# GLA + HGRN2 decoder step: the order of the prologue around the first projection unit

## The reference

```python
def rms_norm(x, w):
    xf = x.astype(jnp.float32)
    y = xf * lax.rsqrt(jnp.mean(xf * xf, axis=-1, keepdims=True) + EPS)
    return (y * w.astype(jnp.float32)).astype(x.dtype)
...
m, s_gla_new, s_hg_new = token_mix(rms_norm(x, norm_mix_pre[l]), w_in[l], ...)
    proj = h @ w_in_l                       # 1024 x 9232, split into 11 parts, one the rank-16 gate
    ... two gated linear recurrences (GLA, 4 heads; HGRN2, 8 heads), gates, merged @ w_out_l
h = x + rms_norm(m, norm_mix_post[l])
f = swiglu(rms_norm(h, norm_ffn_pre[l]), w_ffn_in[l], w_ffn_out[l])
return h + rms_norm(f, norm_ffn_post[l]), s_gla_new, s_hg_new
```

## Time and profile before

| | us |
|---|---|
| Median of 3 runs | 1066.75 (1066.43 to 1067.47) |
| The profiled execution | 1066.12 |
| Its span, first to last instruction | 1064.3 |
| TensorE busy | 1043.1 |
| VectorE busy | 676.6 |
| ScalarE busy | 467.8 |
| POOL busy | 72.4 |

### The profile page before, as it was taken

How to read it: one execution, slowest core, us unless ns; L and a number is a source line. 1 busy time by engine, 2 the same in 40 slices (tenths; PEclk the granted TensorE clock), 3 DMA queues, 4 the chain that set the end, 5 groups by cost and what they waited for, 6 DMA issues and landing times.

```text
span 1064.3 us, 24323 instructions
## 1 busy us (share of the span) xinstructions
PE 1043.1 (98%) x10640; PEld 962.5 (90%) x10640; DVE 676.6 (64%) x982; ACT 467.8 (44%) x720; POOL 72.4 (7%) x89
## 2 busy tenths in 40 slices
PE   7999999999999999999999999799999999999997
PEld 5988999989999899999899878799999999888886
DVE  6266635675526765356664589998888888744544
ACT  6433344622536233445325447544444444533532
POOL 5200003000003000030000020000000000000000
PEclk9999999999999999999999999999999999999999
DMA  6522213622227322245222372123324232422212
GB/s 193 168 72 81 76 55 109 190 62 81 70 62 213 86 62 81 71 124 163 73 61 91 97 250 60 41 80 110 89 83 117 79 106 74 139 80 79 79 60 89
DMA packets 130777, 105.25 MB, mean 99 GB/s; under 512 B 4272, under 2 KB 115888, under 8 KB 130672
## 3 DMA queue, kind: packets, MB, share of 16 engines
q1 hardware_dynamic: 125808, 85.88, 27.4%
q0 software_dynamic: 4864, 17.83, 5.5%
HBM read 91.89 MB, written 11.80 MB: 97 GB/s over the span
## 4 chain that ended last, share of the span: by engine, by line
PE 89%; DVE 5%; ACT 2%; DVEq 1%; issue 1%; ACTq 1%; DMA 0%; POOL 0%; SPq 0%; POOLq 0%
PE ps L282 34%; PE ps L1880 21%; PE ps L1904 13%; PE ps L1171 10%; PE ps L1073 2%; PE ps L1104 1%; PE ps L1094 1%; PE ps L1106 1%; PE ps L1111 1%; PE ps L1087 1%; PE ps L1143 1%; DVE h_t L931 1%; PE ps L1069 1%; PE ps L1131 0%; PE ps L1057 0%
## 5 line engine op out<-in xcount | busy, mean ns | idle before, releaser
L268 ACT ACTIVATE w_hi_t<-w_raw_t 128x1024 fp32r<-128x1024 f32 x73 | 77.2, 1058 | 302.9 <-PE ps L282 218.1
L272 DVE TENSOR_TENSOR w_lo_t<-w_raw_t,w_hi_t 128x1024 fp32r<-128x1024 f32 x73 | 89.7, 1229 | 168.0 <-ACT w_hi_t L268 167.6
L282 PE MATMUL ps<-x_hi,w_lo_t 128*128 128x288 f32 x896 | 195.8, 300 | 0.0
L282 PE MATMUL ps<-x_hi,w_hi_t 128*128 128x288 f32 x896 | 191.5, 295 | 0.0
L282 PE MATMUL ps<-x_lo,w_hi_t 128*128 128x288 f32 x896 | 191.1, 295 | 0.0
L282 PEld LDWEIGHTS ps<-x_hi,w_lo_t 128*128 128x128 f32 x896 | 143.0, 188 | 4.4 <-issue 2.5
L282 PEld LDWEIGHTS ps<-x_lo,w_hi_t 128*128 128x128 f32 x896 | 143.9, 188 | 0.0
L282 PEld LDWEIGHTS ps<-x_hi,w_hi_t 128*128 128x128 f32 x896 | 143.9, 188 | 0.0
L1880 PE MATMUL ps<-x_hi,w_lo_t 128*128 128x288 f32 x264 | 78.1, 296 | 3.5 <-DVE work L1696 2.4
L1880 PE MATMUL ps<-x_lo,w_hi_t 128*128 128x288 f32 x264 | 77.8, 295 | 0.0
L1880 PE MATMUL ps<-x_hi,w_hi_t 128*128 128x288 f32 x264 | 77.8, 295 | 0.0
(11 more groups left out here) (313 smaller groups left out, 2262.7 us busy)
## 6 DMA issues: line engine op xcount, KB each, us to landing
w_raw_t<-in_w_in_dram SPq DMA_DIRECT2D x57, 512.0 KB, 3.7
merged<-in_w_ffn_in_dram SPq DMA_DIRECT2D x22, 512.0 KB, 5.1
w_raw_t<-in_w_ffn_in_dram SPq DMA_DIRECT2D x22, 512.0 KB, 4.5
w_raw_t<-in_w_ffn_out_dram SPq DMA_DIRECT2D x22, 512.0 KB, 3.7
w_raw_t<-in_w_in_dram SPq DMA_DIRECT2D x32, 256.0 KB, 3.8
h_t<-in_x_prompt_dram SPq DMA_DIRECT2D x8, 512.0 KB, 5.3
h_t<-in_state_gla_dram POOLq DMA_DIRECT2D x4, 1024.0 KB, 6.2
h_t<-in_state_hgrn_dram POOLq DMA_DIRECT2D x8, 512.0 KB, 8.0
```

The source lines that it names most:

```text
L268: nc.scalar.activation(w_hi_t[:, u % NSPL, 0:nk, :], w_raw_t[:, u % NRAW, 0:nk, :], ACT.Copy).then_inc(w_hi, 1)
L272: nc.vector.tensor_tensor(w_lo_t[:, u % NSPL, 0:nk, :], w_raw_t[:, u % NRAW, 0:nk, :], w_hi_t[:, u % NSPL, 0:nk, :].bitcast(F32), ALU.subt ...
L282: m = nc.tensor.matmul(out[:, q, :], w[:, u % NSPL, k, :], x(k, q), start=first and i == 0, stop=last and i == len(todo) - 1)
```

## The change

- The norm row is made by eight transposes on TensorE of the gain column, spread to 128 columns, straight into `gain_rows`. VectorE's product and the matmuls with ones go.
- Tile 1 is squared and summed on VectorE (`square_1`, into the same `stat` column), the others still on ScalarE. Tiles 1 and 2 share one Ln and one Exp over two columns.
- Tile 2's rounded copy and remainder are cut in two parts: the first 32 tokens (they complete the first half of 288), and the other 96. There are now six parts (`X_PARTS`), and the banks of the transposed tiles change (`X_BANK`).
- TensorE runs the first half of the low-rank unit after the transposes of tiles 0 to 2, then transposes tiles 3 and 4, then runs the first half of unit 1, the second half of low rank, and the second half of unit 1. Unit 1 leaves the units' loop. One group of four small matmuls stays, ahead of low rank.
- ScalarE and VectorE are written out to match.
- SP issues the two weight loads ahead of tiles 3 and 4.

```diff
+X_BANK = (0, 4, 2, 0, 6)
+X_PARTS = ((0, 0, P), (1, 0, P), (2, 0, HT - 2 * P), (2, HT - 2 * P, P), (3, 0, P), (4, 0, TS))
+NX = len(X_PARTS)
+FIRST_X = 3
...
         for c in range(NT):
+            if c == 3:
+                load_unit(sp, 0, win_v[:, :, GLR:GLR + P])
+                load_unit(sp, 1, win_v[:, :, UNITS[0][0]:UNITS[0][0] + P])
             sp.dma_start(xt[c][0:tok(c), :], xp_v[c] if c < NC else xs_v).then_inc(x_in[c], 16)
-        load_unit(sp, 0, win_v[:, :, GLR:GLR + P])
-        load_unit(sp, 1, win_v[:, :, UNITS[0][0]:UNITS[0][0] + P])
...
+        def main_part(i):
+            act.wait_ge(turned, X_PARTS[i][0] + 1)
+            act.activation(x_hi[:, :, x_cols(i)], x_turned(i), ACT.Copy).then_inc(x_hi_s, 1)
+
+        square_sum(0)
+        inverse_root(0, 1)
+        square_sum(2)
+        act.wait_ge(sum_1, 1)
+        inverse_root(1, 3)
+        main_part(0)
+        square_sum(3)
+        inverse_root(3, 4)
+        main_part(1)
+        main_part(2)
+        square_sum(NC)
+        inverse_root(NC, NT)
+        act.wait_ge(x_lo_s, FIRST_X)
+        main_part(3)
+        main_part(4)
+        main_part(5)
...
-        dve.tensor_tensor(gains, ident[:, :].rearrange("p (o n) -> p o n", o=1).broadcast_to([P, KT, P]),
-                          gain[:, 0, :].rearrange("p (k o) -> p k o", o=1).broadcast_to([P, KT, P]), ALU.mult).then_inc(gain_diag, 1)
+        dve.wait_ge(x_in[1], 16)
+        dve.drain()
+        dve.scalar_tensor_tensor(square_1, xt[1], 1.0, xt[1], ALU.mult, ALU.mult, accum_out=stat[:, 0, 1:2]).then_inc(sum_1, 1)
         dve.wait_ge(gain_row, 1)
...
+        scale_x(0)
+        scale_x(1)
+        scale_x(2)
+        rest_part(0)
+        rest_part(1)
+        rest_part(2)
+        scale_x(3)
+        scale_x(NC)
+        rest_part(3)
+        rest_part(4)
+        rest_part(5)
...
-        for k in range(2):
-            m = nc.tensor.matmul(gain_rows[:, k * HALF:(k + 1) * HALF], ones[:, :], gains[:, 4 * k:4 * k + 4, :], start=True, stop=True)
+        for k in range(KT):
+            m = nc.tensor.transpose(gain_rows[:, k * P:(k + 1) * P], gain[:, 0, k:k + 1].broadcast_to([P, P]), ident[:, :])
         m.then_inc(gain_row, 1)
...
+        def first_unit(q):
+            for k in range(KT):
+                for n, (w, x) in enumerate(((w_lo_t, xh), (w_hi_t, xl), (w_hi_t, xh))):
+                    m = nc.tensor.matmul(proj(1)[:, q, :], w[:, 1, k, :], x(k, q), start=k == 0 and n == 0, stop=k == KT - 1 and n == 2)
+            return m
+
+        turn_x(0)
+        turn_x(1)
+        turn_x(2)
+        pe.wait_ge(x_lo_s, 1)
+        for _ in range(4):
+            nc.tensor.matmul(ps[:, 0, 0:P], ones[:, :], ones[:, :], start=True, stop=True)
+        pe.wait_ge(w_lo, 2)
+        pe.wait_ge(x_lo_s, FIRST_X)
+        low_rank(0)
+        turn_x(3)
+        turn_x(NC)
+        pe.wait_ge(x_lo_s, FIRST_X + 1)
+        pe.wait_ge(w_lo, 3)
+        first_unit(0)
+        pe.wait_ge(x_lo_s, NX)
+        low_rank(1).then_inc(unit_done, 1)
+        first_unit(1).then_inc(unit_done, 1)
```

More of the change, by code:

```diff
@@ L339, in turned_x @@
     def turned_x(c):
-        return ps[:, 2 * (c % 3):2 * (c % 3) + 2, :].rearrange("p a b -> p (a b)").rearrange("p (k t) -> p k t", k=KT)[:, :, 0:tok(c)]
+        bank = X_BANK[c]
+        if c == NC:
+            return ps[:, bank, :].rearrange("p (k t) -> p k t", k=KT)
+        return ps[:, bank:bank + 2, :].rearrange("p a b -> p (a b)").rearrange("p (k t) -> p k t", k=KT)
     def tokens(c):
@@ L552, in _, with square_sum, inverse_root @@
         act.wait_ge(setup, SETUP)
[L553 to L565, removed]
+        def square_sum(c):
+            n = tok(c)
+            act.wait_ge(x_in[c], 16)
+            act.activation(square[0:n, :], xt[c][0:n, :], ACT.Square, accum_out=stat[0:n, 0, c:c + 1])
+        def inverse_root(c0, c1):
+            n = tok(c0)
+            act.drain()
+            act.activation(stat[0:n, 1, c0:c1], stat[0:n, 0, c0:c1], ACT.Ln, scale=1.0 / D, bias=eps_c[0:n, :])
+            act.drain()
+            act.activation(stat[0:n, 1, c0:c1], stat[0:n, 1, c0:c1], ACT.Exp, scale=-0.5).then_inc(squared, c1 - c0)
+        def main_part(i):
[17 more added lines that the diff above has]
+        main_part(5)
         act.wait_ge(small, 16 * 8)
@@ L767, in _, with scale_x, rest_part @@
         dve.drain().then_inc(merged_s, 1)
-        dve.wait_ge(consts, 5)
-        dve.wait_ge(gain_in, 16)
-        dve.tensor_tensor(gains, ident[:, :].rearrange("p (o n) -> p o n", o=1).broadcast_to([P, KT, P]),
-                          gain[:, 0, :].rearrange("p (k o) -> p k o", o=1).broadcast_to([P, KT, P]), ALU.mult).then_inc(gain_diag, 1)
-        dve.wait_ge(gain_row, 1)
[L773 to L782, removed]
+        def scale_x(c):
+            n = tok(c)
+            dve.wait_ge(squared, c + 1)
+            dve.scalar_tensor_tensor(xt[c][0:n, :], xt[c][0:n, :], stat[0:n, 1, c:c + 1], gain_rows[0:n, :],
+                                     ALU.mult, ALU.mult).then_inc(scaled, 1)
+        def rest_part(i):
+            dve.wait_ge(x_hi_s, i + 1)
+            dve.tensor_tensor(x_lo[:, :, x_cols(i)], x_turned(i), x_hi[:, :, x_cols(i)].bitcast(F32), ALU.subtract).then_inc(x_lo_s, 1)
+        dve.wait_ge(x_in[1], 16)
+        dve.drain()
+        dve.scalar_tensor_tensor(square_1, xt[1], 1.0, xt[1], ALU.mult, ALU.mult, accum_out=stat[:, 0, 1:2]).then_inc(sum_1, 1)
+        dve.wait_ge(gain_row, 1)
+        scale_x(0)
[9 more added lines that the diff above has]
+        rest_part(5)
         dve.wait_ge(small, 16 * 8)
@@ L1018, in _, with turn_x @@
     def _(pe):
-        pe.wait_ge(gain_diag, 1)
+        pe.wait_ge(gain_in, 16)
         pe.wait_ge(consts, 5)
-        for k in range(2):
-            m = nc.tensor.matmul(gain_rows[:, k * HALF:(k + 1) * HALF], ones[:, :], gains[:, 4 * k:4 * k + 4, :], start=True, stop=True)
+        for k in range(KT):
+            m = nc.tensor.transpose(gain_rows[:, k * P:(k + 1) * P], gain[:, 0, k:k + 1].broadcast_to([P, P]), ident[:, :])
         m.then_inc(gain_row, 1)
-        for c in range(NT):
+        def turn_x(c):
             n = tok(c)
-            if c >= 3:
-                pe.wait_ge(x_lo_s, c - 2)
-                for _ in range(4):
-                    nc.tensor.matmul(ps[:, 3 * (c - 3), 0:P], ones[:, :], ones[:, :], start=True, stop=True)
             pe.wait_ge(scaled, c + 1)
@@ L1033, in _, with low_rank @@
             m.then_inc(turned, 1)
-        pe.wait_ge(w_lo, 2)
-        for q in range(2):
-            pe.wait_ge(x_lo_s, 3 if q == 0 else NT)
+        def low_rank(q):
             for k in range(KT):
@@ L1040, in _ @@
                                          start=k == 0 and x is x_lo, stop=k == KT - 1 and x is x_hi)
-        m.then_inc(unit_done, 1)
+            return m
[3 more added lines that the diff above has]
+                    m = nc.tensor.matmul(proj(1)[:, q, :], w[:, 1, k, :], x(k, q), start=k == 0 and n == 0, stop=k == KT - 1 and n == 2)
+            return m
+        turn_x(0)
[15 more added lines that the diff above has]
+        first_unit(1).then_inc(unit_done, 1)
         def do_step(j, name):
@@ L1178, in _ @@
                 value_unit(j, n - V0)
-            elif j < G:
+            elif 0 < j < G or j == 0 and n > 0:
                 u = j * NU + n + 1
@@ L1183, in _ @@
                 unit_passes(u, proj(u), xh, xl).then_inc(unit_done, 1)
-            elif n < 3:
+            elif j == G and n < 3:
                 pe.wait_ge(unit_free, UB)
```

10 lines of the change are left out of this document (6 added, 4 removed).

## The result

Over 21 interleaved runs each, the changed kernel has a median of 1068.90 us (1067.51 to 1069.95), the kernel before 1066.86 (1066.18 to 1067.91). The medians lie 2.0 us apart; the ratio, 1.0017 (1.0011 to 1.0023), makes it 1.8 us: a small loss, clear of zero. The time forecast was 1067.4, in a range of 1065.3 to 1069.4.

A forecast was written before the change was run, and what follows sets the result against it. It took TensorE's matmul queue as the bound, so only the second unit's start counts: 29.2 - 28.54 = +0.7 us on the median of 1066.75 gave 1067.4 us, in a range of 1065.3 to 1069.4.

The forecast's parts named there:

- What bounds the kernel: TensorE's matmul queue: gain or loss is the shift of the second unit's start, 28.54 us in the profile before.
- Part 1: Norm row and tile 1's square on VectorE: first scaling at 7.55 instead of 7.66, 0.1 us, worth nothing unless ScalarE keeps up.
- Part 2: ScalarE's order: it idles to 7.5 for tile 2; the first rounded copy runs from 9.95 to 10.95.
- rival B: Clock at 1.2 GHz when low rank starts: its first half costs 2.16 us more, total +2.7, 1069.4; chance 0.22.
- Part 3: Transfers: behind both weight loads tile 3 lands at 12.8 (11.8 to 13.3), where ScalarE wants it at 10.9.
- Part 4: Chain from tile 3: low rank 17.2, unit 1's first half 20.8 (break-even 20.14), then 8.40 us to second unit at 29.2.
- rival C: TensorE: matmuls of unit 1's two halves run slower than whole units, at most 0.2 us; given little chance.
- The cover of the second half: Low rank's second half is wanted at 23.9, its last remainder done at 23.4: wait covered by only 0.5 us.
- low rank's first half, 2.16 us at the full clock: TensorE: low rank's first 16 matmuls, ahead of the transposes of tiles 3 and 4, take 2.16 us.
- the forecast case: Tile 3 landing at 11.8 to 13.3 with the full clock: 1066.4 to 1067.9 us; chance 0.55.
- Rival A: Tile 3 lands before ScalarE wants it at 10.9: second unit at 27.3, -1.2 us, 1065.5; chance 0.18.

The follow-up runs named there:

- e4: The kernel before with only the norm row changed to eight transposes: 1066.82 us, ratio 1.0001.
- e5: The changed kernel with ScalarE's copies of tile 1 and of tile 2's first 32 tokens ahead of tile 3's square: 1066.12 us, ratio 0.9997.
- e2: The changed kernel with SP's transfers in the old order, all token tiles before the two weight loads: 1066.29 us, ratio 0.9995.
- e3: The changed kernel with the old norm row (VectorE's product, two 512-column matmuls with ones): 1069.14 us, ratio 1.0022.
- e7: The changed kernel with the old order of transfers and nine matmuls with ones behind the norm row: 1065.75 us, ratio 0.9992.
- e6: The changed kernel with ten instead of four matmuls with ones ahead of low rank: 1068.20 us, ratio 1.0014.
- e1: The changed kernel with nine matmuls with ones behind the norm row and ten instead of four ahead of low rank: 1067.68 us, ratio 1.0009.
- e9: The same kernel as e7, timed once more on another chip: 1066.07 us, ratio 0.9993.
- e8: e7 with e5's order of copies on ScalarE: 1065.71 us, ratio 0.9992.
- e10: e5 with nine matmuls with ones behind the norm row, new order of transfers kept: 1065.92 us, ratio 0.9995.

## Why the prediction was right, and where its size was off

- **What bounds the kernel.** Right: the shift of the second unit's start, +2.90, is the span's +3.0. Nothing behind it moved between these two profiles (1035.8 and 1035.9 us to the end). Over all profiles here that stretch is 1035.7 to 1036.5 us, so from one execution to another a start tells the time only to within 0.8 us.
- **Part 1.** Right: the new row alone changes nothing (e4). VectorE squares tile 1 as forecast, and the first scaling starts at 7.69 where 7.55 was said.
- **Part 2.** The first copy was put at 9.95 and ran at 11.03. Here the clock was missed: "transposes of tile 0 end 1.1 after its scaling" is a full-clock figure from the earlier trace rows, and at the lower clock they take 1.97 (e5's profile has them apart). It was hidden under the wait for tile 3, as rival B said.
- **Part 3, the decision.** Right: tile 3 lands at 13.13 for 12.8, and ScalarE waits there. One reading was off: POOL first read the second weight load at 13.94, for its rounding, not at 15.06, and only from there does a limit of about 13.3 follow. e2 and e5 show that this wait, by transfer or by the place of the square, is the whole loss.
- **Part 4.** Low rank at 17.58 for 17.2. From there the sum had 2.16 for its first half, 3.65 came (+1.49); 1.4 for the transposes, 1.6 came (22.84 less 21.23); 8.40 to the second unit, 8.60 came, which is rival C below. With 0.38 for the late start these add up to 2.3; between 29.2 and 31.44 lie 2.24. The cover of the second half held: its matmuls follow at 26.11 without a hole.
- **The term that was mis-sized** is "low rank's first half, 2.16 us at the full clock", taken as the likely case at 0.55, with B at 0.22. Both cases are there, in the same kernel: ten runs of 21 lost 1.0 us (forecast 0.7), eleven lost 2.6 (rival B: 2.7). The median is the fastest run of the upper group, so one run the other way would have made it 1068.59. It lies outside the times of the forecast case (1066.4 to 1067.9); what kept it in the range is that the range reached up to B, and where between the two groups a median of such runs falls is luck. B's price was right in total and not in its parts: its 2.0 for the slow first half no run shows, the runs showed 1.49, and the late start, the transposes and unit 1 made up the rest. Its chance should have been about a half.
- **B's cause was wrong.** It was put on the missing long matmuls and a clock that has not risen by 17.2. The clock had risen by 14.23 and fell behind 17.40. e3 has the long matmuls and keeps both groups; e2, e5 and e7, without them, start low rank at full speed. The fall goes with the idle time ahead of low rank: with 2.29 and 2.90 us about half of the runs are slow, with 1.70 (e6) one at most of eleven, and with 1.1 or less there no profile shows it. That its length alone decides isn't shown: in e1 the clock fell earlier on, around holes of 1.21 and 0.87 us, and in e9, the same early work with holes of 2.06 and 0.78, it held. What the change costs besides is the transposes at the lower clock: e7, with the early matmuls, starts low rank 1.25 us sooner than e2. The long matmuls alone don't cure that (e3).
- **Rival A** (tile 3 not late) didn't happen, but e2 makes it happen: -1.2 was forecast, -0.6 measured, and -0.9 with the clock raised early (e7).
- **Rival C** happened, at the 0.2 us that it was given at most. The two halves of unit 1 take 3.27 and 3.20 us (22.84 to 26.11 and 28.24 to 31.44), not 3.12, and with low rank's 2.13 between them that is the 8.60. Whether the three weight tiles of one half are the reason isn't shown.

Open: the link of each group to the speed of low rank rests on one profile in each group, of two kernels (the changed one at 0.997, e3 at 0.999), and on the clock in the records of the other runs. Why the same idle time ends at either clock from run to run isn't shown. Also open is why e5, e8 and e10 keep three or four runs each 0.8 to 2.3 us above their medians; in e10 these have the lowest clocks (0.995 to 0.997), in e5 they have not.

## What to carry to other kernels

A tuned in-order queue is spoiled by one instruction that waits for something new: before moving a transfer back, look at what is ready and stands behind its reader on that engine, and move the reader too. An order that takes work from the shadow ahead of a queue into the queue must first earn it back: here low rank had to start before 20.14 - 2.16 - 1.6 = 16.4 us to break even in the profile, and a start at 15.4, 2.6 us sooner than before, brought the second unit forward by 0.8. An idle hole just ahead of dense matmuls has a second price, the clock, which may come in only half of the runs, so look at every run's time and clock and not at one profile.
